# Norm sums and per-token decay columns as 128x32 tiles, and a unit's wait for the inverse moved behind its first eight transposes

## What is computed

```python
kk = l2norm(rwkv_heads(k * rwkv_k_k))                      # norm over 64 channels
bonus = jnp.sum(rh * kh * rwkv_r_k, axis=-1, keepdims=True) * vh
q = l2norm(gdn_heads(q)) * GDN_HEAD_DIM ** -0.5            # norms over 128 channels
k = l2norm(gdn_heads(k))
gc = jnp.cumsum(g, axis=-1)                                # per head, in chunks of 64 frames
decay = jnp.exp(jnp.where(causal, gc[..., :, None] - gc[..., None, :], -jnp.inf))
q_dec = q * jnp.exp(gc)[..., None]
k_dec = k * jnp.exp(gc[..., -1:] - gc)[..., None]
tmat = lax.linalg.triangular_solve(eye + lower, ...)       # the "inverse" of a chunk
```

## Time and profile before

| | us |
|---|---|
| median of 3 runs | 2353.65 (2353.60 to 2360.31) |
| profiled execution | 2358.39 |
| its span, first to last instruction | 2356.5 |
| TensorE busy | 2161.3 (92%) |
| VectorE busy | 1414.1 (60%) |
| ScalarE busy | 1086.9 (46%) |
| mean granted TensorE clock | 0.948 |

### The profile page before, as it was taken

The page is one execution under the profiler, slowest core; times in us unless marked ns, Lnnn a source line. Parts: engine busy times, 40 slices in busy tenths (PEclk is TensorE's granted clock), DMA queues, the critical chain, the costliest instruction groups (busy, mean ns, idle before and its releaser), DMA issues. The chain is left out here.

```text
span 2356.5 us, 51465 instructions
## 1 busy us (share of the span) xinstructions
PE 2161.3 (92%) x19523; PEld 1862.1 (79%) x19523; DVE 1414.1 (60%) x2772; ACT 1086.9 (46%) x2019; POOL 158.2 (7%) x277
## 2 busy tenths in 40 slices
PE   5699999999999999999999966939999999999995
PEld 5698888888888888888888854838888888878884
DVE  3276687778677766867776754444554544444444
ACT  4354555545554545555454533344444444434443
POOL 2000110110011011101101110000000000000000
PEclk8699999999999999999999966969999999999998
DMA  4654545444444545444544304426655555545452
GB/s 114 155 143 116 138 111 132 123 125 125 115 116 123 129 113 139 113 113 123 130 114 113 87 5 185 154 90 197 195 182 192 181 192 182 174 165 191 178 184 101
DMA packets 388239, 327.32 MB, mean 139 GB/s; under 512 B 15360, under 2 KB 328160, under 8 KB 381408
## 3 DMA queue, kind: packets, MB, share of 16 engines
q1 hardware_dynamic: 376304, 319.16, 46.5%
q10 hardware_dynamic: 11760, 5.41, 0.9%
HBM read 322.44 MB, written 2.10 MB: 138 GB/s over the span
## 5 line engine op out<-in xcount | busy, mean ns | idle before, releaser
L1489 DVE TENSOR_TENSOR wlo<-wr,whi 128x1024 fp32r<-128x1024 f32 x296 | 362.4, 1225 | 436.0 <-ACT whi L1484 436.0
L232 PE MATMUL ps<-hi,xh 128*128 128x384 f32 (+1 forms) x1600 | 581.7, 364 | 42.8 <-DVE lo L218 24.4
L234 PE MATMUL ps<-hi,xl 128*128 128x384 f32 (+1 forms) x1600 | 548.9, 343 | 0.0
L233 PE MATMUL ps<-lo,xh 128*128 128x384 f32 (+1 forms) x1600 | 548.1, 343 | 0.0
L1484 ACT ACTIVATE whi<-wr 128x1024 fp32r<-128x1024 f32 x296 | 313.5, 1060 | 493.2 <-PE ps L1502 484.9
L218 DVE TENSOR_TENSOR lo<-raw,hi 128x768 fp32r<-128x768 f32 (+1 forms) x400 | 378.1, 964 | 147.6 <-ACT hi L213 144.0
L213 ACT ACTIVATE hi<-raw 128x768 fp32r<-128x768 f32 (+1 forms) x400 | 328.1, 834 | 245.8 <-PE ps L234 235.4
L232 PEld LDWEIGHTS ps<-hi,xh 128*128 128x128 f32 x1600 | 311.1, 194 | 76.4 <-issue 47.7
L1498 PE MATMUL ps<-whi,xh 128*128 128x512 f32 x832 | 328.1, 394 | 20.5 <-DVE wlo L1489 20.5
L1502 PE MATMUL ps<-whi,xl 128*128 128x512 f32 x832 | 326.9, 393 | 0.0
L1500 PE MATMUL ps<-wlo,xh 128*128 128x512 f32 x832 | 326.5, 392 | 0.0
(11 more groups left out here) (284 smaller groups left out, 2396.1 us busy)
## 6 DMA issues: line engine op xcount, KB each, us to landing
raw<-in_w_in SPq DMA_DIRECT2D x294, 512.0 KB, 5.5
wr<-in_ffn_w_gate SPq DMA_DIRECT2D x44, 1024.0 KB, 5.2
wr<-in_ffn_w_up SPq DMA_DIRECT2D x44, 1024.0 KB, 5.2
wr<-in_ffn_w_down SPq DMA_DIRECT2D x22, 2048.0 KB, 7.7
wr<-in_w_out SPq DMA_DIRECT2D x16, 1024.0 KB, 5.2
xt<-in_x SPq DMA_DIRECT2D x1, 2048.0 KB, 8.0
x<-in_x SPq DMA_DIRECT2D x1, 2048.0 KB, 15.8
out_x<-y SPq DMA_DIRECT2D x1, 2048.0 KB, 7.0
```

The costliest lines, as they stand in the source:

```text
L232: nc.tensor.matmul(o, xh[:, kc, xs], hi[q % QBUF][:, k, 0:w], start=kc == 0, stop=False)
L233: nc.tensor.matmul(o, xh[:, kc, xs], lo[q % QBUF][:, k, 0:w], start=False, stop=False)
L234: last = nc.tensor.matmul(o, xl[:, kc, xs], hi[q % QBUF][:, k, 0:w], start=False, stop=kc == KC - 1)
L1489: nc.vector.tensor_tensor(wlo[s.par][:], src, whi[s.par][:].bitcast(F32), ALU.subtract).then_inc(s.lo, 1)
```

## The change

There are three edits. The decay columns: the two products with one column each, for each frame tile, become products with the two frame tiles' columns side by side (`ub[:, :, 1]`), done for four groups of 32 output rows (`QUADS`), so that each has 32 columns of weights; the output columns are now ordered by kind and then by frame tile, and `ege` and `gcc` read them in that order. The norm sums: each of the eight products becomes four, of 32 columns of weights each. The wait for "xf1" moves from before "tr1" to before "tr3".

```diff
                 if prev:
-                    wait(pe, A, "xf1", u, 1)
                     wait(pe, V, "tk1", u, 1)
                 for name, todo in (("tr1", ...), ("tr2", ...), ("tr3", ...)):
+                    if prev and name == "tr3":
+                        wait(pe, A, "xf1", u, 1)
...
                 for t in range(NT):
-                    mm(ps[:, 1, cols(t)], ub[:, t, 1:2].to_broadcast([P, P]), cum_up)
-                    mm(ps[:, 1, T + 2 * t:T + 2 * t + 1], cum_up, ub[:, t, 1:2])
-                    last = mm(ps[:, 1, T + 2 * t + 1:T + 2 * t + 2], strict_lo[:], ub[:, t, 1:2])
+                    last = mm(ps[:, 1, cols(t)], ub[:, t, 1:2].to_broadcast([P, P]), cum_up)
+                for k, m in enumerate((cum_up, strict_lo[:])):
+                    for q in QUADS:
+                        last = mm(ps[q, 1, T + 2 * k:T + 2 * k + 2], m[:, q], ub[:, :, 1])
                 E.step("decay", last)
...
                 for t in range(NT):
-                    o = ps[:, 2, 8 * t:8 * t + 8]
-                    mm(o[:, 0:2], sq[:, 0, cols(t)], headsel[:])
-                    mm(o[:, 2:3], sq[:, 1, cols(t)], ones[:])
-                    mm(o[:, 3:4], sq[:, 2, cols(t)], ones[:])
-                    last = mm(o[:, 4:6], prod[:, cols(t)], headsel[:])
+                    for at, left, right in ((0, sq[:, 0, cols(t)], headsel), (2, sq[:, 1, cols(t)], ones),
+                                            (3, sq[:, 2, cols(t)], ones), (4, prod[:, cols(t)], headsel)):
+                        for q in QUADS:
+                            last = mm(ps[q, 2, 8 * t + at:8 * t + at + right.shape[1]], left[:, q], right[:])
...
-                fn("ege", ege[:].rearrange("p a b -> p (a b)"), ps[:, 1, T:T + 4], ACT.Exp)
+                fn("ege", ege[:].rearrange("p t w -> p w t"), ps[:, 1, T:T + 4].rearrange("p (w t) -> p w t", w=2), ACT.Exp)
...
-                V.step("gcc", nc.vector.tensor_copy(gcc[:], ps[:, 1, T:T + 4:2]))
+                V.step("gcc", nc.vector.tensor_copy(gcc[:], ps[:, 1, T:T + 2]))
```

## The result

The changed kernel is slower: median 2435.9 us (2434.49 to 2438.43), beside 2356.74 for the kernel before in the same runs, a ratio of 1.0343 (95% interval 1.0322 to 1.0363). The forecast was 2332, faster; the time lies 87 us above the range.

What follows compares the result with a forecast made beforehand. TensorE's program order was taken as the bound. 1.6 us a unit over 14 units, 22.4, plus 1.5 for unit 0 and 2.4 for unit 15, made 26.3 us off 2358.39: 2332 us, range 2316 to 2349.

Steps and rivals of the forecast that it cites:

- A: Mixing stage: shorter block as summed, clock falls in half of the units, 2332 us; chance 0.42.
- F: Small products: column tiles using all 128 rows don't run side by side, 42 ns a record, slower, 2372 us; chance 0.08.
- the idle time before the transposes unchanged: Loop's top: TensorE's idle 1.31 us before the transposes stays, a sign that the forecast is right.
- The block of decay and norm products: TensorE in the mixing stage: 1.5 us instead of 3.21, with small records at 10 ns each.
- Rival D: Small products: records follow each other at 25 ns, the block takes 2.7 us, 2335 us in all; chance 0.08.
- the new wait for ScalarE: Before quantum 24: 1 us of the block's gain becomes TensorE waiting for ScalarE's projection copy; quantum starts 0.73 us earlier.
- VectorE: Reader of the norm sums moves from 715.55 to about 714.5, its chain ends at 717.7; nothing is late.
- The moved wait: Transposes at the loop's top: one register step goes, counted 0, at most a tenth of a microsecond a unit either way.
- The clock: TensorE behind the norm sums: half-speed falls costing 1.75 us each, taken to occur in half of the units.
- B: TensorE's clock behind the norm sums: every unit still falls, gain 13 us, 2345 us; chance 0.20.
- C: TensorE's clock behind the norm sums: no unit falls, gain 39 us, 2319 us; chance 0.12.
- E: Clock over the units: it takes the gain back, only the ends are won, 4 us, 2354 us; chance 0.10.

Runs made afterwards that it cites:

- loop_tiles: The changed kernel, but unit 0 in front of the loop has the full products, so small tiles in the loop: 2333.04 us, ratio 0.9903.
- pad20: The changed kernel with five tiny unused products (20 instructions) in front of unit 0: 2333.25 us, ratio 0.9899.
- wait_only: The kernel before with only the wait moved to the third group of transposes, full products everywhere: 2352.61 us, ratio 0.9986.

## Why the prediction was wrong

**The step that failed** is a term that the sum hasn't got. Of the code it says "What goes is one register step ahead of the transposes. I count 0", and it counts added instructions by their time on TensorE alone: 80 small records, 0.8 us. That the tiles add 112 instructions ahead of the loop, which move the loop's code against the blocks in which it is fetched, and 112 in the loop, it does not ask, and none of the rivals A to F has it. One of the signs at its end does lie at the loop's top, "the idle time before the transposes unchanged", and it is this one that failed: over all transposes the idle time is 78.5 us in place of 17.0, though ahead of the first four of a unit it stays near 1.3. The idle time "put down to issue" at shape changes was read as a drain of 0.25 us; the same word at the loop's top covered a wait for code.

What the term is worth: the kernel after less loop_tiles, which has all the tiles of the loop and no stall, is 2435.9 - 2333.0 = 102.9 us. Stalls: 62.5 in 13 units. The clock behind them: 13 x 6.8 us at half speed, of which TensorE works 5.04 of 6.80, half of it lost, 13 x 2.5 = 33. The clock behind the norm sums falls in 14 of the units 0 to 14 and not in 9: 5 x 1.75 = 9. Together about 104.

**Right, step by step**, by the kernel after at its own place, and by loop_tiles and pad20 for the times:
- The block of decay and norm products: forecast 1.5 us, measured 1.63; small records forecast at 10 ns, measured 11.5. Rival D (25 ns) and F (42 ns) are out. The row that decided was the 32x32 one; that of the 128x64 tiles was no guide. The Trainium skill's page "TensorE: Matmul & The Clock Gate" has the floor of about 25 ns ("Wait — 56ns, not 53.3ns?") and the rule on row groups ("Part 3: Packing small matmuls — row/col tiling"); both, at the times that the prediction set beside them (2.7 and 4.05 us), give a longer block than the 1.63 us of these rows.
- The quantum: forecast 0.13 us behind the copy, so measured; the new wait for ScalarE forecast as 1 us, measured 0.82.
- VectorE: nothing late, as forecast; `nrm` right behind the second split.
- The moved wait: forecast 0, at most 0.1 us a unit; wait_only is 0.14% faster (0.04 to 0.24%), 3 us or 0.2 us a unit. Small, of the right sign for the gain allowed, and a little larger.
- The clock: half of the units forecast. In loop_tiles it fell behind the norm sums in 8 of the units 1 to 14, in pad20 in 8 as well. In loop_tiles the units without a fall last 79.27 us on average (forecast 79.34), those with one 81.08. Two of its stretches, one kept, one fallen:

```profile
301.90:304.20 2.30, 2.30 (x12) 2.05 (x12) 1.77 (x11) 1.07 (x3) 0.00 (x0) 1.00 0.00 0
382.00:385.30 3.30, 3.30 (x11) 3.01 (x10) 1.37 (x8) 0.58 (x3) 0.00 (x0) 0.52 0.00 0
```

That refutes B, C and E. A's sum was 2332 and the two kernels without the stop take 2333.0 and 2333.3: the mechanism of the tiles was right, and a second one, four times its size, sat 28 us upstream of the place I looked at.

That the sums meet within 1 us is in part luck. The forecast took 26.3 us off a single execution of 2358.39; the medians beside the two kernels are 2355.61 and 2357.38, and they gain 22.6 and 24.1. One slip is in the rows: the last unit's transposes begin at 1345.18 and not at 1346.39, so a unit took 81.71 us before and not 81.79, and 14 units gain 19.6 us in loop_tiles where the sum has 22.4.

## What to carry to other kernels

Instructions are not free where they lie: where a change adds or removes some ahead of or inside a hardware loop, look in the profile after for an "issue" idle a few instructions behind the loop's top, in the turns entered by a branch and not in the first. The number of blocks does not show it: of the kernels with the stop one has 161, as before, and the others 175. If the idle time is there, move the block's end with a few unused instructions ahead of the loop (here 20 gave 4.2%). Keeping large transfers from starting at the loop's top should help too, since thinner ones did; a kernel that only moves them was not run. A result that comes out wrong by more than the changed place can hold is looked for over the whole turn, by the groups of idle time, before the change itself is blamed.

## What the runs showed of the hardware

- A block of code that ends some ten instructions behind a loop's top makes TensorE stand for 4.8 us a turn, 2.2 to 2.9 with the weight loads thinned, 4.1 when it ends 16 instructions later and up to 1.4 when 64 later. From the start of its transfer to the next matmul it is 2.3 to 2.8 us in the kernel after. What makes the sequencer ask for the block, and so why it asks late behind a branch, no run here shows.
- Float32 products with all 128 rows and 32 columns on four column groups take 11.5 ns a record (80 in 0.92 us), though each load lasts nearly ten times as long:

```profile
L674 PEld LDWEIGHTS ps<-headsel,sq x256: 106/109/113, 142.9 to 1446.0; 128*32 128x32 f32 x128
```

- Twelve unused 128-column products in a stretch of small work kept the clock at 1.00 in all of units 1 to 14, where it fell in 8 without them, and gave 7 us net (2333.25 to 2326.62).
